# Decode-attention scores: taken by VectorE from the key banks instead of by score columns on TensorE

## The reference, cut to what matters

```python
def mla_keys(latent, w_uk, w_uv, k_norm_nope):
    ...
    kn = rms_norm((c @ w_uk).reshape(bsz, s, MLA_HEADS, NOPE_DIM), k_norm_nope)
    ...
def mla_scores(qn, qr, kn, kr):
    s = jnp.einsum('bqhd,bkhd->bhqk', qn, kn) + jnp.einsum('bqhr,bkr->bhqk', qr, kr)
    return s.astype(jnp.float32) * MLA_SCALE
```

## Time and profile before

| | |
|---|---|
| three timed runs | 1430.38, 1432.32, 1432.69 us; median 1432.32 |
| profiled execution, its own time | 1431.02 us |
| its span in the trace | 1429.2 us |
| PE busy | 1413.9 us (99%) |
| VectorE busy | 800.7 us (56%) |
| ScalarE busy | 872.3 us (61%) |
| GpSimd busy | 220.9 us (15%) |
| page loop | about 101 to 1106 us |

### The profile page before, as it was taken

How to read it: one execution, slowest core, us unless ns; L and a number is a source line. 1 busy time by engine, 2 the same in 40 slices (tenths; PEclk the granted TensorE clock), 3 DMA queues, 4 the chain that set the end, 5 groups by cost and what they waited for, 6 DMA issues and landing times.

```text
span 1429.2 us, 30941 instructions
## 1 busy us (share of the span) xinstructions
PE 1413.9 (99%) x11108; PEld 1339.3 (94%) x11108; DVE 800.7 (56%) x1651; ACT 872.3 (61%) x2908; POOL 220.9 (15%) x115
## 2 busy tenths in 40 slices
PE   9999999999999999999999999999999999999998
PEld 7889998999999999999989999889999999999998
DVE  5764444556446564555645555645334667777543
ACT  5544778677666686576965667766774453444332
POOL 3011111211122111112321111131231000000000
PEclk9999999999999999999999999999999999999999
DMA  9541325543345543355333463344734565555551
GB/s 283 172 119 31 65 50 118 143 123 80 72 100 129 124 89 87 75 139 122 87 74 92 109 141 68 72 70 91 177 76 152 175 236 177 177 177 176 177 179 59
DMA packets 263731, 173.77 MB, mean 122 GB/s; under 512 B 165465, under 2 KB 212089, under 8 KB 263577
## 3 DMA queue, kind: packets, MB, share of 16 engines
q1 hardware_dynamic: 263266, 171.53, 46.4%
q10 hardware_dynamic: 318, 0.33, 0.1%
HBM read 132.22 MB, written 6.74 MB: 97 GB/s over the span
## 4 chain that ended last, share of the span: by engine, by line
PE 92%; ACT 4%; DVE 2%; issue 1%; DMA 0%; ACTq 0%; POOL 0%; DVEq 0%
PE ps L2044 17%; PE ps L2045 16%; PE ps L2046 16%; PE ps L2479 6%; PE ps L2480 6%; PE ps L2481 6%; PE ps L2082 2%; PE ps L2135 2%; PE ps L2427 2%; PE ps L2428 2%; PE ps L2136 2%; PE ps L2429 2%; PE ps L2137 2%; PE ps L1918 2%; ACT ksq L868 1%
## 5 line engine op out<-in xcount | busy, mean ns | idle before, releaser
L2044 PE MATMUL ps<-ukh,cTh 128*128 128x384 f32 (+1 forms) x1536 | 505.6, 329 | 3.9 <-ACT ksq L868 2.4
L2045 PE MATMUL ps<-ukl,cTh 128*128 128x384 f32 (+1 forms) x1536 | 491.7, 320 | 0.0
L2046 PE MATMUL ps<-ukh,cTl 128*128 128x384 f32 (+1 forms) x1536 | 491.2, 320 | 0.0
L868 ACT ACTIVATE ksq<-ps 128x128 f32<-128x128 f32 x1024 | 269.3, 274 | 181.8 <-PE ps L2046 179.8
L2044 PEld LDWEIGHTS ps<-ukh,cTh 128*128 128x128 f32 x1536 | 289.9, 189 | 22.7 <-issue 18.2
L2045 PEld LDWEIGHTS ps<-ukl,cTh 128*128 128x128 f32 x1536 | 289.2, 188 | 0.9
L2046 PEld LDWEIGHTS ps<-ukh,cTl 128*128 128x128 f32 x1536 | 288.7, 188 | 0.0
L719 POOL TENSOR_TENSOR rk<-kss,mhalf 128x32 f32<-128x32 f32 x32 | 180.4, 5636 | 456.7 <-DVE kss L1708 456.7
L868 ACT ACTIVATION_READ_ACCUMULATOR ksq<-ps 128x1 f32 x1024 | 209.2, 204 | 0.0
L853 ACT ACTIVATE cTr<-turned 128x1024 uint16<-128x1024 uint16 x126 | 174.1, 1382 | 5.9 <-PE ps L2072 3.7
L1049 ACT ACTIVATE wh<-wraw 128x2048 fp32r<-128x2048 f32 x44 | 84.3, 1916 | 131.4 <-PE ps L2481 126.9
(11 more groups left out here) (518 smaller groups left out, 2536.6 us busy)
## 6 DMA issues: line engine op xcount, KB each, us to landing
clat<-cache_mla SPq DMA_DIRECT2D x128, 256.0 KB, 2.6
wraw<-w_in SPq DMA_DIRECT2D x16, 1024.0 KB, 5.1
wraw<-w_up SPq DMA_DIRECT2D x16, 1024.0 KB, 5.2
wraw<-w_down SPq DMA_DIRECT2D x16, 1024.0 KB, 5.1
braw<-w_in SPq DMA_DIRECT2D x24, 512.0 KB, 4.1
crope<-cache_mla SPq DMA_DIRECT2D x128, 32.0 KB, 2.4
sst<-state_gdn SPq DMA_DIRECT2D x32, 128.0 KB, 3.5
gdn_sample<-sst SPq DMA_DIRECT2D x32, 128.0 KB, 2.0
```

Of the source, the lines that this page charges most:

```text
L868: i = nc.scalar.activation(ksq[:, P * h:P * h + P], ps[:, k % 3, P * h:P * h + P], ACT.Square, accum_out=kss[:, n // 4 % 2, n % 4, h0 + h: ...
L2044: mm(out, cTh[:, n % 2, c], ukh[:, c, cols], start=c == 0, stop=False)
L2045: mm(out, cTh[:, n % 2, c], ukl[:, c, cols], start=False, stop=False)
L2046: i = mm(out, cTl[:, n % 2, c], ukh[:, c, cols], start=False, stop=c == 3)
```

## The change

1. The 8 score columns go. A page is two banks of 512 columns: 24 matmuls of 512. The three banks are used in turn as before, so a bank is used again three groups of matmuls later, that is one and a half pages on.
2. VectorE multiplies each bank by the query, broadcast to all partitions (`qb`, 128 x 512, loaded by a DMA from a small DRAM tensor), into `prod` (`scored`), and sums 2 x 4 heads of 128 (`score_sums`), one reduction of 1024 columns a page. A bank is now free only when VectorE has multiplied it (`prod_done`). In VectorE's order the second half of page n-1 and its sum stand behind `split_lo(n + 1)` in page n's first half, the first half of page n stands at the end of page n.
3. ScalarE's copy of the score columns, `query_slot`, `first_scores`, the transposes of `w_uk`, the products with them and the turning of their result (`qcol`) go. The query itself is turned by 8 small transposes instead (`qrow`).
4. The rotary keys are turned by a DMA of their own for each group (`split_rope` on VectorE, `rope_turn` on SP, 512 16-bit columns) and no longer on TensorE; ScalarE's copy reads 512 16-bit columns instead of 256 float32.
5. The power -1/2 is taken per page (128 x 8) with the scaling ahead of it, both on GpSimd (`page_roots`); VectorE's L1708 goes.
6. `cTr` is two pages deep instead of four; each square on ScalarE signals for itself and waits for the one three before.

The core of the diff:

```diff
-        KG = [(slice(0, 384), 0, 3, False), (slice(384, 768), 3, 3, False), (slice(768, 1024), 6, 2, True)]
+        KG = [(slice(0, 512), 0), (slice(512, 1024), 4)]
...
+            def rope_turn(gg):
+                sp.wait_ge(S("rplanes_ready"), gg + 1)
+                wait(sp, "rope_ready", gg)
+                sp.dma_start(rturned[:].bitcast(U16).rearrange("p (x n) -> p x n", n=P), rplanes[:].bitcast(U16), transpose=True).then_inc(S("rope_turned"), 16)
...
+            def query_half(h):
+                s_, j = divmod(h, 2)
+                if h >= 3:
+                    sp.wait_ge(S("prod_done"), 32 * ((h - 3) // 2) + 31 + (h - 3) % 2)
+                sp.dma_start(qb[h % 3][:], scratch[s_:s_ + 1, LAT * j:LAT * j + LAT].to_broadcast([P, LAT])).then_inc(S(f"qb_landed{h % 3}"), 16)
...
+                if i == 1:
+                    sp.wait_ge(S("a_read"), a_count("qrow1"))
+                    sp.dma_start(scratch, qrow[0:NS].rearrange("s g n -> s (g n)")).then_inc(S("scratch_landed"), 16)
+                    sp.wait_ge(S("scratch_landed"), 16)
+                    query_half(0)
+                    query_half(1)
...
-            def group(gg, y):
-                g.wait_ge(S("ms_ready"), gg + 1)
-                nc.gpsimd.tensor_tensor(rk[:, y], kss[:, y], mhalf[:], ALU.pow).then_inc(S("rk_ready"), 1)
+            def page_roots(n):
+                x = kss[:, n // 4 % 2, n % 4]
+                g.wait_ge(S("squared"), 8 * n + 8)
+                nc.gpsimd.tensor_scalar(x, x, 1.0 / 128, EPS, ALU.mult, ALU.add).then_inc(S("ms_ready"), 1)
+                g.wait_ge(S("ms_ready"), n + 1)
+                if n >= 8:
+                    g.wait_ge(S("s_half"), n // 4 - 1)
+                nc.gpsimd.tensor_tensor(rk[:, n // 4 % 2, n % 4], x, mhalf[:, 0], ALU.pow).then_inc(S("rk_ready"), 1)
...
+            def scored(n, j):
+                k, h = 2 * n + j, 2 * (n // 16) + j
+                if n % 16 == 0:
+                    v.wait_ge(S(f"qb_landed{h % 3}"), 16 * (h // 3 + 1))
+                v.wait_ge(S("squared"), 4 * k + 4)
+                wait(v, "page_scored", n)
+                V.tensor_tensor(prod[:, j], ps[:, k % 3], qb[h % 3][:], ALU.mult).then_inc(S("prod_done"), 1)
+
+            def score_sums(n):
+                v.wait_ge(S("prod_done"), 2 * n + 2)
+                V.tensor_reduce(sparts[:, n // 4 % 2, n % 4], prod[:].rearrange("p j (h d) -> p (j h) d", d=P), AX, ALU.add).then_inc(S("page_scored"), 1)
...
             for n in range(NT):
                 g, t = n // 4, n % 4
                 beside(2 * n)
                 if n + 1 < NT:
                     split_lo(n + 1)
...
+                if n:
+                    scored(n - 1, 1)
+                    score_sums(n - 1)
...
                 beside(2 * n + 1)
                 if n + 3 < NT:
                     split_planes(n + 3)
+                if n:
+                    scored(n, 0)
+                if t == 3 and g + 1 < NG:
+                    split_rope(g + 1)
...
                 if chunks[0] == 0:
                     pe.wait_ge(S("ct_lo"), n + 1)
-                    wait(pe, "ksq_ready", k - 2)
+                    wait(pe, "prod_done", k - 2)
...
-                if t == 2:
-                    rope_columns(g)
                 beside(2 * n)
                 key_chunks(n, 0, (0, 1, 2, 3))
                 key_chunks(n, 1, (0,))
...
                 key_chunks(n, 1, (1, 2, 3))
-                key_chunks(n, 2, (0, 1, 2, 3))
```

More of the change, by code:

```diff
@@ L722, in group @@
                 nc.gpsimd.partition_all_reduce(smax[:].rearrange("p t h -> p (t h)"), ssc[:, y].rearrange("p t h -> p (t h)"), P, RMAX).then_inc(S("smax_ready"), 1)
-            for gg in range(NG):
-                group(gg, gg % 2)
+            for n in range(NT):
+                if n:
+                    page_roots(n - 1)
+                if n % 4 == 1 and n > 1:
+                    group_max(n // 4 - 1, (n // 4 - 1) % 2)
+            page_roots(NT - 1)
+            group_max(NG - 1, (NG - 1) % 2)
         @block.scalar
@@ L869, in squares @@
-                i.then_inc(S("ksq_ready"), 1)
+                if j == 0:
+                    wait(act, "rk_ready", n - 7)
+                for h in range(4):
+                    m = 4 * k + h
+                    wait(act, "squared", m - 2)
+                    i = nc.scalar.activation(ksq[m % 3], ps[:, k % 3, P * h:P * h + P], ACT.Square, accum_out=kss[:, n // 4 % 2, n % 4, h0 + h:h0 + h + 1]).then_inc(S("squared"), 1)
             def turned_rope(gg):
-                act.wait_ge(S("rope_done"), gg + 1)
+                act.wait_ge(S("rope_turned"), 16 * (gg + 1))
@@ L1330, in front_dve @@
                 if i == 1:
+                    for g in range(2):
+                        V.tensor_copy(qrow[0:NS, g], a_bank(f"qrow{g}")[0:NS]).then_inc(S("a_read"), 1)
+                if i == 2:
                     tmp = rtmp[:, 0, 0:4 * NS].rearrange("p (a s) -> p a s", s=NS)
@@ L1343, in front_dve @@
                     v.wait_ge(S("pool_clear"), 2)
-                    for g in range(2):
-                        V.tensor_copy(qeff[:, :, :, 4 * g:4 * g + 4], a_bank(f"qcol{g}").rearrange("p (c q x) -> p x c q", c=4, q=4)[:, 0:NS]).then_inc(S("a_read"), 1)
                     qx = qrope[:].rearrange("p s (j a b) -> p j a b s", j=2, b=2)
@@ L2065, in rope_scores @@
                 k.then_inc(S("rope_scored"), 1)
-            def first_scores():
-                pe.wait_ge(S("ct_raw"), 4)
-                pe.wait_ge(S("qeff_ready"), 1)
-                for t in range(4):
-                    for c in range(4):
-                        k = mm(ps[:, B_ROPE, 384 + H * t:384 + H * t + H], cTr[:, c, tokens(t)], qeff[:, 0, c, :], start=c == 0, stop=c == 3)
-                k.then_inc(S("first_scores"), 1)
             def weigh(gg):
@@ L2420, in z_unit @@
                     elif i == 0:
-                        pe.wait_ge(S("ksq_ready"), 3 * (NT - 1) + j + 1)
+                        pe.wait_ge(S("prod_done"), max(k for k in range(2 * NT - 3, 2 * NT) if k % 3 == j) + 1)
                     if i >= 2 and i % 2 == 0:
```

204 lines of the change are left out of this document (75 added, 129 removed).

## The result

The changed kernel takes 1448.93 us (median of 4, 1448.38 to 1448.96) and the kernel before, beside it, 1432.51: a ratio of 1.0117, interval 1.0104 to 1.0130. It is 16.4 us slower. The profiled executions differ by 17.9 us.

A forecast was written before the change was run, and what follows sets the result against it. The prediction took TensorE as the bound (busy 1413.9 of 1429.2 us). Savings of 26.3 us and losses of 35.9 from VectorE's late answers, on the median 1432.3, gave 1441.9; it predicted 1442 us, range 1414 to 1464.

The forecast's parts named there:

- Columns: Key products on TensorE: 24 matmuls of 512 columns a page save 0.062 us a page, 7.9 us in all.
- Rotary transposes: TensorE's rotary-key transposes, two for each of 32 groups: removing them saves 9 us, bounds 7 and 11.
- Small score products: Small score matmuls of the first pages: removing them saves 3.9 us plus 1.5 for the lowered clock, 5.4 us.
- the start: First pages: VectorE's first product waits for query halves passed through DRAM, costing TensorE 2.5 us, bounds 0 and 5.
- The ring of the projections: Second and fourth pairs' projections: VectorE's chain takes 9.4 us against TensorE's page of 8.7; 12.4 us lost.
- State steps: Steps 34 to 46 of each pair: VectorE in time except where t = 1; 1.5 us a pair, 6 us lost.
- the normalisation: Steps 16 to 21 of each pair: additions of 5 us meet about 2 us of idle; 3.2 a pair, 13 us lost.
- The bank's way back: TensorE's wait for a bank VectorE must multiply first: 2.5 us in the first pages, 0.5 at the loop's end.
- B: Rival, faster: VectorE's existing waits swallow the additions, leaving 8 us of stalls; 1414 us, chance 0.30.
- C: Rival, heavier: the sum costs 1.6 us, or normalisation stalls lower TensorE's clock; 1470 us, chance 0.12.
- D: Rival: GpSimd becomes the bound, a power of 8 columns taking 5.6 us; 1460 to 1600 us, chance 0.06.

The follow-up runs named there:

- fused kernel: The changed kernel with product and sum in one VectorE instruction for each head, eight a page in place of two products and a sum: 1426.61 us (ratio 0.9958).

## Why the prediction was right, and where it was off

The sign, the mechanism and most of the places held: TensorE was given less to do, VectorE's answers came late at the pairs, and the loss outweighed the gain. The forecast was 1442, measured 1448.93; both sides of its sum were too small, the savings by 7.5 us and the costs by 15.8, from the ledger. These errors partly cancel, and that is luck: the measured savings (33.8) with the forecast costs (35.9) would have given a change of 2 us, which is within the noise.

**Columns: mis-sized.** The step taken for 512 columns, 0.2339, came from the front's value products; the key products run at 0.2291. A page is then 24 x 0.2291 = 5.50 us against 5.68, which is 0.18 for each page and not 0.06; the ledger's quiet pages say 0.16. The statement that fewer, longer matmuls gain nothing was wrong: 0.1756 for 384 columns is 0.457 ns a column, 0.2291 for 512 is 0.447. A difference of two large numbers was taken from rows of two different places in the program.

**Rotary transposes: mis-sized.** The gain was 3.3 to 6.1 us and not 9. The chain's 0.22 us per pair was right: in the kernel before without them the pages in which they stood are 0.22 us shorter in the median and 6.2 us in all, in the changed kernel 0.18 and 5.8. The 2 us put on top for the change-over aren't there, and in the kernel before 2.5 us came back in other pages, with 2 us more of waits on TensorE. Small score products and the start were right within 2 us.

**The ring of the projections: right in its length.** For the second pair the prediction gave 9.4 us from answer to answer, 0.6 more with the maxima (t = 3). The rows, on VectorE:

```profile
445.98 0.43 DVE L1503 TENSOR_TENSOR qkv<-ps,rx 128x264 f32<-128x264 f32 x1 [2.13 <-PE ps L2136]
...
456.05 0.43 DVE L1503 TENSOR_TENSOR qkv<-ps,rx 128x264 f32<-128x264 f32 x1 [1.73 <-PE ps L2136]
...
459.15 0.69 DVE L1280 TENSOR_TENSOR prod<-ps,qb 128x512 f32<-128x512 f32 x1
459.87 1.22 DVE L1284 TENSOR_REDUCE sparts<-prod 128x8 f32<-128x1024 f32 x1
461.01 1.22 DVE L1334 TENSOR_TENSOR bwl<-braw,bwh 128x1024 fp32r<-128x1024 f32 x1
...
465.61 0.43 DVE L1503 TENSOR_TENSOR qkv<-ps,rx 128x264 f32<-128x264 f32 x1 [2.18 <-PE ps L2136]
```

From 445.98 to 456.05, the page with t = 3 in which TensorE waited 1.45 us for `bwl`, are 10.07 us, the forecast's 9.4 + 0.6. From 456.05 to 465.61 are 9.56, but there TensorE did not wait: `bwl` ends at 461.01 + 1.22 = 462.23, and the next projection starts at 462.40, so this is TensorE's own page and the ring is 0.2 shorter, 9.4 again. TensorE waits for `bwl` at 452.84 (1.45), 473.47 (1.97) and 484.45 (0.46), and in the fourth pair at 837.30, 857.91 and 877.43 (0.73, 2.42, 1.45); in the first and third pair never, as forecast. It cost 9.9 and not 12.4, because TensorE's own page there was 9.0 to 9.8 us in three of four cases and not 8.7: only pages with t = 1 and t = 3 waited.

**State steps: a chain overlooked.** This is the cost that was furthest off. "VectorE answers once in each half page, in time except where t = 1 puts 1.5 us ahead" overlooked step 44, a second chain of reciprocal square roots as long as that of step 16 (4.4 us). Four pairs lost 16.4 us there and not 6, with waits for the bank of 1.83, 1.11, 3.00 and 0.94 us behind the chains and the clock's dips behind three of these. With the normalisation (17.1 for 13) the places of the two chains hold 33.5 of the 51.7 us lost.

**The bank's way back was priced at the start and the end alone,** 3 us in all. It is 25.1 us in 21 waits, and 10.8 in 9 even where the additions are nearly gone. Most of the rest is a name and not a cause: whichever of bank, weights, roots and page comes last in VectorE's order is waited for, and the time stays the same (waits of 45.8 us from 84 us to the loop's end in the change, 40.3 with the sum later, 45.6 with the product ahead of the roots). That does not hold for every order: with the product early everywhere it is 62.4, and the time rises.

**The rivals.** B, that VectorE's waits swallow the additions, is half right: VectorE's wait for ScalarE shrank from 124.8 us to 85.7, and three quarters of the sum's time did vanish. It was to decide if product and sum in the ring took under 1.2 us: they took 1.86 and the time rose; in the fused kernel the half page that stands there takes 4 x 0.21 = 0.85, and the time came out below that of before. C gave the sum 1.6 us, which it doesn't cost (1.22), but its other half came true: the clock fell behind waits of 0.9 to 4.5 us, for 7.8 us beyond before, where it had priced four dips at 6. The Trainium skill (TensorE: Matmul & The Clock Gate, "HAM oscillation") has an engine that stalls between bursts lose its clock as well. The trace agrees in part: 0.83 or 0.84 in five windows at such waits, but 1.00 around the waits of 1.85 us at 520 and of 2.42 at 858:

```profile
850.00:860.00 10.00, 7.58 (x42) 6.28 (x41) 8.64 (x18) 5.88 (x20) 0.18 (x1) 1.00 0.63 154
860.00:870.00 10.00, 10.00 (x63) 8.79 (x63) 7.16 (x12) 5.68 (x20) 0.98 (x3) 1.00 0.38 83
```

So the length of a single wait does not decide it here. The weight given to the opposite, from one wait of 1.12 us with a clock of 1.00, was too much. D fell: a power of 8 columns takes 1.71 us, and with the roots taken by group the time is the same. In 16 of 32 groups GpSimd stands 7.4 us ahead of the first scaling behind a maximum with nothing to wait for, 118.9 us in all, hidden as forecast. The Trainium skill (GPSIMD Engine Reference, "Instruction dispatch") has the first call of a newly loaded routine pay about 6 us; the place fits, the size is somewhat larger.

What stays open: how much of the 51.7 us is the clock itself. The windows give 7.8 us more than before, but a dip also delays what comes behind it. ScalarE's part is open too: it is nearly full ahead of the longest stall, and VectorE waits for it there. A ScalarE with less to do, a product that doesn't wait for its squares, and a sum on another engine weren't tried.

## What to carry to other kernels

Work moved from the bounding engine to a half idle one costs more than its share says, where the idle one serves in a fixed order and within deadlines of a page: here a quarter of each microsecond of the sum came back as time, though it was busy for 76% of the span. Look for its longest unbroken chains (here 4.4 us of reciprocal square roots, twice a pair), add the new work to just those pages, and expect an order to rename a wait, not to end it (four orders changed nothing here, a fifth cost 32 us); shortening the work (here one instruction for product and sum) is what pays. Take both sides of a small difference from the same place of the program.

## What the hardware showed that was not expected

- A multiply of 128 columns that also writes a sum from its accumulator takes VectorE 0.21 us from start to start, its read of the accumulator (82 ns) hidden under the next one: 1.7 us for 1024 columns multiplied and summed, against 2.5 in three long instructions. Here eight short instructions were cheaper than three long ones.
- The granted clock was 0.83 or 0.84 over ten microseconds at single waits of 1.8 to 4.5 us between long busy stretches, and once at two of 0.9; it stayed at 1.00 at others of 1.85 and 2.42 us.
- 512-column products run at 0.2291 us among the key products and at 0.2339 among the front's, which are of the same shape.
